# Eight instead of five Strassen tile pairs in each feed-forward block, six of them in neighbouring couples

## The reference

```python
def swiglu(u, w_gate, w_up, w_down):
    return (jax.nn.silu(u @ w_gate) * (u @ w_up)) @ w_down

for l in range(DEPTH):                                   # DEPTH = 2
    f = swiglu(rms_norm(h, ffn1_pre_g[l]), ffn1_w_gate[l], ffn1_w_up[l], ffn1_w_down[l])
    h = h + 0.5 * rms_norm(f, ffn1_post_g[l])
    ...                                                  # the mixer
    f = swiglu(rms_norm(h, ffn2_pre_g[l]), ffn2_w_gate[l], ffn2_w_up[l], ffn2_w_down[l])
    h = h + 0.5 * rms_norm(f, ffn2_post_g[l])
```

## Time and profile before

| | |
|---|---|
| median of the runs | 2000.99 us |
| the profiled execution | 2001.3 us, span 1999.5 us |
| granted TensorE clock | 0.999 of full |
| PE busy | 1986.0 us, 99% of the span |
| DVE, ACT, POOL busy | 913.9, 824.6, 1029.3 us (46%, 41%, 51%) |
| DMA | 88 GB/s mean, q1 busy for 26.6% of 16 engines' span |

### The profile page before, as it was taken

One profiled execution on the slowest core, in us unless ns is written; L12 is line 12 of the kernel. 1 busy time (PEld: TensorE's weight loads), 2 busy tenths in 40 slices (PEclk: granted clock), 3 DMA queues, 4 the chain that ended last, 5 costly groups with the idle time before them and its releaser, 6 DMA issues.

```text
span 1999.5 us, 35699 instructions
## 1 busy us (share of the span) xinstructions
PE 1986.0 (99%) x15084; PEld 1909.5 (96%) x15084; DVE 913.9 (46%) x1433; ACT 824.6 (41%) x1318; POOL 1029.3 (51%) x1257
## 2 busy tenths in 40 slices
PE   9999999999999999999999999999999999999998
PEld 9999999999899999999999999999998998888887
DVE  6663310478546765210076542103785467642102
ACT  6433222465555533232264332224555465332321
POOL 3655554576315655454375554544763256564551
PEclk9999999999999999999999999999999999999999
DMA  4224332132201223332122333321322112333321
GB/s 167 86 94 125 103 102 86 67 96 80 64 33 43 85 85 127 100 117 88 57 75 85 96 117 111 102 84 62 101 82 65 33 54 74 109 124 107 116 73 43
DMA packets 48479, 175.76 MB, mean 88 GB/s; under 512 B 5184, under 2 KB 9408, under 8 KB 48320
## 3 DMA queue, kind: packets, MB, share of 16 engines
q1 hardware_dynamic: 48176, 173.40, 26.6%
q10 hardware_dynamic: 144, 0.10, 0.0%
HBM read 171.38 MB, written 2.10 MB: 87 GB/s over the span
## 4 chain that ended last, share of the span: by engine, by line
PE 98%; DVE 1%; ACT 1%; DMA 0%; issue 0%; SPq 0%; DVEq 0%
PE ps L1803 97%; PE ps L2184 1%; DMA h<-in_x 0%; DVE osb L1751 0%; ACT xh L829 0%; DVE xl L1761 0%; DVE tail_step L1295 0%; PE ps L2063 0%; DVE probT L1719 0%; ACT prob L1151 0%; DVE small L1728 0%; DVE h L1300 0%; ACT tmp L1187 0%; ACT xh L1202 0%; DVE wlo L1329 0%
## 5 line engine op out<-in xcount | busy, mean ns | idle before, releaser
L747 POOL TENSOR_TENSOR wlo<-raw,whi 128x256 fp32r<-128x256 f32 (+2 forms) x1148 | 944.0, 854 | 726.2 <-ACT whi L799 723.6
L1803 PE MATMUL ps<-xh,whi 128*128 128x264 f32 (+2 forms) x2680 | 645.3, 296 | 3.2 <-DVE xl L1334 1.5
L1803 PE MATMUL ps<-xl,whi 128*128 128x264 f32 (+2 forms) x2680 | 641.7, 295 | 0.0
L1803 PE MATMUL ps<-xh,wlo 128*128 128x264 f32 (+2 forms) x2680 | 640.8, 295 | 0.0
L1803 PEld LDWEIGHTS ps<-xh,whi 128*128 128x128 f32 x2680 | 445.0, 188 | 17.4 <-DVE wlo L1329 2.3
L799 ACT ACTIVATE whi<-raw 128x1024 fp32r<-128x1024 f32 (+3 forms) x329 | 356.0, 1083 | 255.7 <-PE ps L1803 221.6
L1803 PEld LDWEIGHTS ps<-xl,whi 128*128 128x128 f32 x2680 | 443.7, 188 | 11.4
L1803 PEld LDWEIGHTS ps<-xh,wlo 128*128 128x128 f32 x2680 | 443.6, 189 | 10.5
L1803 PE MATMUL ps<-hidh,whi 128*128 128x264 f32 (+2 forms) x1276 | 313.6, 296 | 0.0
L1803 PE MATMUL ps<-hidl,whi 128*128 128x264 f32 (+2 forms) x1276 | 312.5, 295 | 0.0
L1803 PE MATMUL ps<-hidh,wlo 128*128 128x264 f32 (+2 forms) x1276 | 312.4, 295 | 0.0
(11 more groups left out here) (218 smaller groups left out, 2332.8 us busy)
## 6 DMA issues: line engine op xcount, KB each, us to landing
raw<-in_ffn_up SPq DMA_DIRECT2D x88, 512.0 KB, 3.7
raw<-in_ffn_down SPq DMA_DIRECT2D x64, 704.0 KB, 4.0
raw<-in_ffn_gate SPq DMA_DIRECT2D x87, 512.0 KB, 3.6
raw<-in_w_in SPq DMA_DIRECT2D x28, 512.0 KB, 3.5
raw<-in_w_out SPq DMA_DIRECT2D x16, 512.0 KB, 3.6
raw<-in_w_q SPq DMA_DIRECT2D x8, 384.0 KB, 3.2
out_t<-h SPq DMA_DIRECT2D x16, 128.0 KB, 1.8
h<-in_x SPq DMA_DIRECT2D x2, 528.0 KB, 5.7
```

The source lines that it names most:

```text
L747: ins = nc.gpsimd.tensor_tensor(w_lo(n)[:, at], raw[:, r, at], w_hi(n)[:, at].bitcast(F32), ALU.subtract)
L1803: return nc.tensor.matmul(o, w, x, start=start, stop=stop)
```

## The change

Three things are edited. `STRASSEN` goes from (5, 7, 9, 11, 13) to (5, 7, 8, 10, 11, 13, 14, 16). To let pairs up to m = 16 use the token sums, `t_hi` and `t_lo` get new places: the parts of the `whi`, `wlo` and `raw` slots beyond 1024 columns, which gate and up tiles don't use, and the last five instead of eight chunks of the hidden activations. And the order on DVE and ACT is changed where two Strassen pairs stand side by side.

```diff
-STRASSEN = (5, 7, 9, 11, 13)
+STRASSEN = (5, 7, 8, 10, 11, 13, 14, 16)
...
-        t_hi = sb_at("t_hi", arena + (FC - DC) * CH, [P, KH, T_SUMS, HALF], F32R)
-        t_lo = sb_at("t_lo", arena + (2 * FC - DC) * CH, [P, KH, T_SUMS, HALF], F32R)
...
+        T_HI = [whi[:, :, spare], raw_spare[:, :, spare], four(FC - 5, 0), four(FC - 3, 0)]
+        T_LO = [wlo[:, :, spare], last, four(FC - 5, 1), four(FC - 3, 1)]
...
                     if m in STRASSEN:
-                        part_copy(m)
+                        if m - 1 not in STRASSEN:
+                            part_copy(m)
                         for i in range(3):
                             hi(n[i] + RING)
-                        silu(m)
-                        hi(n[3] + RING)
+                        if m + 1 in STRASSEN:
+                            hi(n[3] + RING)
+                            silu(m)
+                            part_copy(m + 1)
+                        else:
+                            silu(m)
+                            hi(n[3] + RING)
                         hid_hi(m)
...
                         strassen_sums(m, 0)
-                        sums(nxt[1])
-                        low(nxt[0])
-                        sums(nxt[2])
-                        low(nxt[1])
-                        strassen_sums(m, 1)
-                        strassen_sums(m, 2)
-                        low(nxt[2])
+                        if m + 1 in STRASSEN:
+                            sums(nxt[2])
+                            sums(nxt[3])
+                            strassen_sums(m, 1)
+                            low(nxt[1])
+                            strassen_sums(m, 2)
+                        else:
...
                         strassen_sums(m, 3)
                         gate(m)
                         up(m)
-                        sums(nxt[3])
+                        if m + 1 not in STRASSEN:
+                            sums(nxt[3])
                         hid(m)
                         low(nxt[3])
                         hid_lo(m)
                         continue
...
                     hid(m)
+                    if m + 1 in STRASSEN and m + 2 in STRASSEN:
+                        sums(TILES_OF[b, m + 2][1])
                     low(nxt[1])
                     hid_lo(m)
```

More of the change, by code:

```diff
@@ L129, in build_program @@
     assert FC % 2 == 0 and FC >= 6
-    assert FC - DC > max(STRASSEN) and FC - DC - 4 > min(STRASSEN) > 4
+    assert FC - 5 > max(STRASSEN) and FC - 9 > min(STRASSEN) > 4 and FH >= DC + 3
+    assert not any(m + 1 in STRASSEN and m + 2 in STRASSEN for m in STRASSEN)
     tiles = []
@@ L312, in build_program @@
         f_ffn = sb_at("f_ffn", xl_at, [P, DC, T], F32)
+        raw_at = base[0]
         raw = sb("raw", [P, RING, MAXT * P], F32)
@@ L329, in build_program, with four, t_half, t_one @@
         hidl = sb_at("hidl", arena + FC * CH, [P, FC, T], F32R)
-        t_hi = sb_at("t_hi", arena + (FC - DC) * CH, [P, KH, T_SUMS, HALF], F32R)
-        t_lo = sb_at("t_lo", arena + (2 * FC - DC) * CH, [P, KH, T_SUMS, HALF], F32R)
-        t_in = sb_at("t_in", arena + (FC - DC - 4) * CH, [P, 2, T], F32)
-        t_sum = sb_at("t_sum", arena + (FC - DC - 2) * CH, [P, T_SUMS, HALF], F32)
+        hid_all = sb_at("hid_all", arena, [P, 2, FC, T], F32R)
+        raw_spare = sb_at("raw_spare", raw_at, [P, RING, MAXT * P], F32R)
+        spare = slice(DC * P, DC * P + HALF)
+        def four(first, which):
+            return hid_all[:, which, first:first + 2, :].rearrange("p a (i t) -> p (a i) t", i=2)
+        last = hid_all[:, :, FC - 1, :].rearrange("p a (i t) -> p a i t", i=2)
+        T_HI = [whi[:, :, spare], raw_spare[:, :, spare], four(FC - 5, 0), four(FC - 3, 0)]
+        T_LO = [wlo[:, :, spare], last, four(FC - 5, 1), four(FC - 3, 1)]
+        def t_half(part, k, nt):
+            at = part[k]
+            if at is last:
+                return at[:, :, :, 0:nt]
+            return at[:, :, 0:nt]
+        def t_one(part, k, i, nt):
+            at = part[k]
+            if at is last:
+                return at[:, i // 2, i % 2, 0:nt]
+            return at[:, i, 0:nt]
+        def t_whole(k, nt):
+            at = t_sum[:, :, 0:nt]
+            return at.rearrange("p (a i) t -> p a i t", i=2) if T_LO[k] is last else at
+        t_in = sb_at("t_in", arena + (FC - 9) * CH, [P, 2, T], F32)
+        t_sum = sb_at("t_sum", arena + (FC - 7) * CH, [P, T_SUMS, HALF], F32)
         off = [arena]
@@ L989, in sum_hi @@
                     nt = span(trim, 0)[1]
-                    nc.scalar.activation(t_hi[:, k, :, 0:nt], t_sum[:, :, 0:nt], ACT.Copy).then_inc(t_hi_ready, 1)
+                    nc.scalar.activation(t_half(T_HI, k, nt), t_sum[:, :, 0:nt], ACT.Copy).then_inc(t_hi_ready, 1)
                 def part_copy(m):
@@ L1431, in t_sums, with t_high @@
                     nc.vector.tensor_tensor(t4, b21, t2, ALU.subtract).then_inc(t_sum_ready, 1)
+                def t_high(k, nt):
+                    at = t_half(T_HI, k, nt).bitcast(F32)
+                    return at.rearrange("p (a i) t -> p a i t", i=2) if T_LO[k] is last else at
                 def t_low(k):
@@ L1435, in t_low @@
                     nt = span(trim, 0)[1]
-                    nc.vector.tensor_tensor(t_lo[:, k, :, 0:nt], t_sum[:, :, 0:nt],
-                                            t_hi[:, k, :, 0:nt].bitcast(F32), ALU.subtract).then_inc(t_lo_ready, 1)
+                    nc.vector.tensor_tensor(t_half(T_LO, k, nt), t_whole(k, nt), t_high(k, nt), ALU.subtract).then_inc(t_lo_ready, 1)
                 def sums(n):
@@ L1506, in ffn @@
                         strassen_sums(m, 0)
-                        sums(nxt[1])
-                        low(nxt[0])
-                        sums(nxt[2])
-                        low(nxt[1])
-                        strassen_sums(m, 1)
-                        strassen_sums(m, 2)
-                        low(nxt[2])
+                        if m + 1 in STRASSEN:
[5 more added lines that the diff above has]
+                        else:
+                            sums(nxt[1])
+                            low(nxt[0])
+                            sums(nxt[2])
+                            low(nxt[1])
+                            strassen_sums(m, 1)
+                            strassen_sums(m, 2)
+                            low(nxt[2])
                         strassen_sums(m, 3)
@@ L1854, in sums @@
                 def sums(i):
-                    return lambda k: (t_hi[:, k, i, 0:nt], t_lo[:, k, i, 0:nt])
+                    return lambda k: (t_one(T_HI, k, i, nt), t_one(T_LO, k, i, nt))
                 slot_in(n[0])
```

## The result

The changed kernel takes 2023.55 us, the median of four runs (2022.76 to 2023.8); the kernel before took 2001.04 beside it (four runs). The ratio is 1.0111, 95% interval 1.0099 to 1.0124: slower, as forecast, but by 22.5 us where 13.8 were worked out, and above the range that ended at 2021. The profiled execution took 2023.56 with a span of 2021.8; that of before had 1999.5. So 22.3 us of the span are to be found.

A forecast was written before the change was run, and what follows sets the result against it. PE was taken as the bound, with 98% of the chain. Savings of 17.4 us, waits of 30.3 and 0.9 for the statistics gave +13.8 on the span of 1999.5: forecast 2014.5 us, range 2003 to 2021.

The forecast's parts named there:

- The saving, 1.52 and 1.23 a pair: PE, each ordinary pair turned into Strassen: 1.52 us less, 1.23 in block 5; 17.4 us saved in all.
- When DVE can start, 4.21: Start of two neighbouring Strassen pairs: DVE starts the second's sums at 4.21 us, once its up load has landed.
- Four collisions of 2.1 in all: Where a couple begins: four DVE instructions wait in turn for POOL's on the shared SBUF port, +2.1 us a couple.
- 30.3 us of waits: PE waits for the bank gate(m) frees: 2.3 us in nine couples (blocks 0, 2, 3), 3.2 in three (block 5).
- behind zero: Time counted from when DVE sees the end of the tile before a couple of neighbouring Strassen pairs.
- 15.4 was worked out: Block 5 couples: DVE's chain through gate(m) ends and frees PE's bank at 15.4 us after the tile before.
- 12.2: Block 5 couples: PE asks for the second pair's bank at 12.2 us after the tile before, giving a 3.2 wait.
- The copy on ACT costs nothing in its new place: Second pair's copy comes 1.1 us after gate(m); PE asks for it 1.8 us after the bank, so no cost.
- The statistics, 0.9: Block 4: PE's statistics wait for the bank pair DVE still reads for the last query tile, 0.9 us.
- a wait costs its own length, and PE's matmuls keep 0.122 us: Sign on PE: if Strassen matmuls come at another pace than 0.122 us, the first step is wrong.
- The case that came nearest, 2022.3: Couples: 1024-column low part also meets POOL's next batch, +0.6 each; block 5 delay carries over; +21.3, chance 0.12.

The follow-up runs named there:

- six_apart: The changed kernel with STRASSEN at (5, 7, 9, 11, 13, 15), one more pair a block than before and none adjacent: 1996.4 us, ratio 0.9977.
- pool_one: The changed kernel with POOL making the low part of each couple's second pair's first slot by one instruction instead of four, three quarters left out: 2004.53 us.
- twelve_waits: The kernel before with only 12 PE waits added, before gate tiles m = 15, 18 and 21 of each feed-forward block: 2035.18 us, ratio 1.017.
- sums_later: The changed kernel with DVE's s13 sums of a couple's second pair moved behind the first pair's first addition: 1998.74 us, ratio 0.9991.

## Why the prediction was wrong in size, step by step

- *The saving, 1.52 and 1.23 a pair.* Right: six_apart gave 3.8 where 5.8 less 1.8 was due.
- *When DVE can start, 4.21.* Measured 4.18 in the first couple: POOL is through at 91.71 and SP issues the up load at 91.74, as read from the earlier trace rows. In later couples it starts as late as 5.98 in block 0 and 6.40 in block 5, which was not forecast.
- *Four collisions of 2.1 in all.* Right in the first couple (1.15 + 1.22 + 1.22 + 1.23, against four times 0.69: 2.06), and pool_one took three away with POOL's instructions. The Trainium skill (SBUF — State Buffer, Who interferes with whom) has the port pair as an exclusive lock held for a whole instruction; pool_one agrees, one instruction left and one slowed.
- *30.3 us of waits.* Nearly right in sum: against their pace PE's matmuls lose 29.4 us in the couples, 2.37 a couple in the blocks 0, 2 and 3 (2.3 forecast) and 2.7 a couple in block 5 (3.2 forecast). The wait at L1525, a bank that I had not asked about, is a part of this and does not come on top: in the first couple PE loses 0.3 there and 2.0 at the gate, and 2.3 was forecast, since the gate ends when DVE is through. That the couples are so alike was not foreseen. DVE starts 4.17 to 6.40 behind zero and one to four of its instructions are slowed, yet the gate ends between 14.89 and 15.22 in all twelve: a later start meets fewer of POOL's instructions. The latest start is in the first couple of block 5, 0.3 later than worked out:

```profile
1719.40 0.69 DVE L1437 TENSOR_TENSOR tmp<-ps,rs_in 128x512 f32<-128x512 f32 x1 [1.74 <-PE ps L1850]
...
1725.80 0.95 DVE L1488 TENSOR_TENSOR raw<-raw 128x512 f32<-128x512 f32 x1 [4.98 <-DMA raw<-in_ffn_up]
1726.67 0.68 DVE L1489 TENSOR_TENSOR raw<-raw 128x512 f32<-128x512 f32 x1
...
1733.93 0.69 DVE L1429 TENSOR_TENSOR tmp<-ps,rs_in 128x512 f32<-128x512 f32 x1
```

```profile
1723.38 2.82 POOL L775 TENSOR_TENSOR wlo<-raw,whi 128x256 fp32r<-128x256 f32 x4 [1.27 <-ACT whi L827]
```

POOL ends at 1726.20, and only L1488 meets it. Here the late load and the missing collisions cancelled: the gate ends at 15.22, and 15.4 was worked out. That the sum came out in such couples is in part luck. The rest of block 5's difference is that PE comes to ask some 0.2 later than 12.2.
- *The copy on ACT costs nothing in its new place.* Right: putting it back costs 5.6.
- *The statistics, 0.9.* Right (L1679).
- *What failed: a wait costs its own length, and PE's matmuls keep 0.122 us.* That was never a term of the sum, only a line under what would make it wrong. The clock fell behind five of the twelve couples' waits and cost 7.4 us. That, with 1.5 of small gaps and 0.4 less of waits (30.8 where 30.3 + 0.9 stood), is the 8.5 between +13.8 and +22.3. The trace of before could have warned only by what it lacks: nowhere in its feed-forward loops does PE wait (its longest wait is 1.7 us, once, for the mask L1226 in the opening, and not the 1.5 that I had read), and so none of its rows shows what PE does behind a wait of 2 us. The range should have had a bound for it.
- *The case that came nearest, 2022.3, is not what happened.* It took 0.6 more in each couple from the low part of 1024 columns, which would meet POOL's next batch. It does meet it (POOL's is from 102.07 on), but takes 1.28 to 1.33 where 1.226 is its length, 0.1 more. Its nearness to the measured time is luck.

It stays open which waits bring the clock down. In the changed kernel all twelve gate waits are alike (6.2 us for the three of each block by the weight loads' rows), yet five had the stretch behind them; nothing read from the traces sets those five apart.

## What to carry to other kernels

On a PE that never waits, price a new wait at its length and give it a second term for the clock behind it: here twelve waits of 2 us and the small ones beside them cost 29 us, and then 7 more. Before an instruction that waits for a load is put into a queue, look at what stands behind it that frees a bank for PE: moving it took about 25 us off, and one long low part on DVE and a high part on ACT, moved together, took 9 more, so that a loss of 22.5 us became a gain of 11.4. What each of the last two gave is not known. A "98% busy" PE says nothing of either; its share of the chain and the matmuls per window do.

## What the hardware did that I had not expected

- Behind a PE wait of 2.0 to 2.2 us, or from its last 0.3 us on, the granted clock was 0.50 in five of twelve places, in two different kernels (changed: 7.4 us lost, twelve_waits: 7.1). The matmuls of 264 columns then start 0.22 us apart, not 0.122.
- 192 matmuls of no use, put into the waits, made the kernel 7.2 us faster (2023.55 to 2016.4).
- While POOL was in its low parts, DVE's instructions with two SBUF operands were slowed whatever they computed: sums_later moved the four collisions on to L1488, L1489, L1492 and L1497 (1.05, 1.22, 1.11, 1.04) without removing one. POOL's four took 4.17 instead of 2.83.
